# Two transformer blocks on one core: the experts' end reordered with down weights in column halves, and the first projection unit loaded by itself

## The chip, the cores and the metric

The kernel runs on one core of a Trainium2 chip, in float32, as one program of five instruction streams: TensorE (PE in the profile, PEld for its weight loads), VectorE (DVE), ScalarE (ACT), GpSimd (POOL) and SyncE (SP), which here only issues DMAs and waits. The metric is the device time of one execution in microseconds (us), the median of several runs.

## What is computed

```python
def first_block(x, ...):                      # x: 512 tokens x 1024
    h = rms_norm(x, g_attn);  proj = h @ w_in # 1024 x 3072
    o_da = diff_attention(...);  o_sb = stick_breaking(...)
    x = x + concat(o_da, o_sb) @ w_o
    h2 = rms_norm(x, g_ffn)
    return x + hier_moe(h2, wg, bg, we, be, w1, w3, w2)

def hier_moe(h, ...):                         # 4 groups x 8 experts = 32, top 2 of a group
    ...                                       # per expert, on its tokens:
    ys = (silu(xb @ w1[e]) * (xb @ w3[e])) @ w2[e]    # 1024 -> 512 -> 1024
    ys = ys * gate;  out[token] += ys

def second_block(x, c, ctx, ...):             # ctx: 256 x 1024
    h_lat = modulate(rms_norm_2(x, g_pre_mix), sh_m, sc_m)
    p_lat = h_lat @ w_in_2                    # fourier | q_a | kv_a | k_rope
    h_ctx = modulate(rms_norm_2(ctx, g_pre_mix), csh_m, csc_m)
    p_ctx_kv = h_ctx @ w_in_2[:, KV_COL:]     # keys and values of the context
    ...                                       # latent attention, fourier mix, w_out, swiglu
```

## The kernel before

Every weight matrix is cut on the host into items of [128, 4096] float32 (2 MiB, 16 KB a partition). SyncE loads them in one fixed order (`items`) into eight slots: five of the tile `ring`, two halves of `B3` (in the traces `B`), and `TO`. A small loop at the top of the program decides for each item which slot it takes (`where`); before a load SyncE waits until the item that lay in the slot was used (`consumed`). Lines 338 to 365 are that loop, lines 431 to 455 `consumed`.

**The start.** SyncE issues the four parts of x, the parameters PRM and then items 0 to 3. Item 0 is the first quarter of `w_in` that is used; four units of 128 columns are taken from it. For each unit ScalarE rounds the weights (`proj_high`, UH), VectorE takes the rest (`proj_low`, UL), and TensorE multiplies (three products per chunk of 128 rows). The activations are split in the same way: ScalarE makes HH, VectorE HL, from the transposed x in PSUM. `proj_high(0)` waits for the whole item and for PRM.

**The experts.** Each expert x has 64 places for tokens. Its up product takes 16 calls with `w13` (items (x,0) and (x,1), each half of the 1024 rows), two calls at a time side by side in the array. ScalarE makes the silu, VectorE the product (`hidden`), TensorE turns it (`turn`, L957), VectorE copies it (`hidden_cols`, HT). Experts go in pairs p: `down_pair(p)` multiplies experts 2p and 2p+1 with their `w2` items (x,2), 16 calls into PSUM banks 6 and 7, each call 64 rows of one expert. ScalarE and VectorE scale and split the result (YH, YL), and `combine(p, k)` adds it with a one-hot matrix to rows of tokens 128k to 128k+127; VectorE adds that to X (`added`, L2154). `down_pair(p)` stands behind the up product of expert 2p+2, and `combine(p, 0..3)` between the chunks of expert 2p+3's.

**The end of the experts.** After expert 31's up product come its turn, a branch for tokens that found no place (`passes`, not taken here), `down_pair(15)` and `combine(15, 0..3)`. Then the second block starts: keys of the context (`acc` with W1 and `small_keys`, from item `i1`, the first part of `w_in_2`), the norms of X by ScalarE (`row_norm`), and `turn_x(k)`, which turns X and scales it by the norm, in between the small products of the context. With `hT` complete the query projection starts (L57, `ps<-B,ring 128x512`).

The loads end with the `w2` items of experts 30 and 31, then the two parts of `w_in_2` with `w_b_2` in between. Most matmuls are recorded at L57 in the helper `mm`; the tiles tell them apart.

Of the kernel before, what the change touches and what calls it, by code (L numbers as in the profile page):

```python
# [19 lines left out]
NE = 32  # L20
# [5 lines left out]
LN_EXP = 6  # L26
N_PARAM = 927
# [50 lines left out]
def body(nc, ctx, I, out):  # L78
# [95 lines left out]
    PROJ = (3, 4, 5, 2, 0, 1)  # L174
# [73 lines left out]
    WX2 = WX[2].rearrange("p (c n) -> p c n", c=4)  # L248
# [68 lines left out]
    for x in range(NE):  # L317
        use += [(x, 0), (x, 1)]
        if x >= 2 and x % 2 == 0:
            use += [(x - 2, 2), (x - 1, 2)]  # L320
    use += [(NE - 2, 2), (NE - 1, 2)]
    item_of = {u: I_EXP + n for n, u in enumerate(use)}
    for x, part in use:
        items.append(I["w2"][x] if part == 2 else I["w13"][2 * x + part])
    I_IN2 = len(items)
    items += [I["w_in_2"][:, 0:3328], I["w_b_2"], I["w_in_2"][:, 3328:7424]]
# [7 lines left out]

    where, before, landed = [], [], []
# [3 lines left out]
    for i in range(len(items)):  # L339
        if i < I_EXP:  # L340
            line_up = [early[i]]
        if i == I_EXP:
            line_up = [1, 2, 0, 4, 3, NSLOT + 2, NSLOT + 1, NSLOT]
        if I_EXP + 8 <= i <= I_IN2:
            line_up.sort(key=freed.get)
        if i == I_IN2:
            line_up = [k for k in line_up if k < 3]
        if i == I_EXP + 57:
            line_up.remove(NSLOT + 2)
        k = line_up[0]  # L350
        if I_IN2 - 4 <= i < I_IN2:
            k = next(q for q in line_up if (q in (4, NSLOT + 1)) == (i >= I_IN2 - 2))
        line_up.remove(k)
        line_up.append(k)
        if I_EXP <= i < I_IN2:
            x, part = use[i - I_EXP]
            freed[k] = 8 * (x // 2) + 10 if part == 2 else 4 * x + part
# [14 lines left out]
    i1, iw, i0 = I_IN2, I_IN2 + 1, I_IN2 + 2  # L372
# [9 lines left out]
    x_in = [sem(f"x{t}_in") for t in range(4)]  # L382
    prm_in, cst_in, ohb_in, brow_out, tbr_in, zero_out = (
# [27 lines left out]
    up_half = sem("up_half")  # L411
# [30 lines left out]
    def consumed(j):  # L442
# [6 lines left out]
        if j < I_IN2:  # L449
            x, part = use[j - I_EXP]  # L450
            return (up_half, up_mm, dn_mm2)[part], x // 2 + 1 if part == 2 else x + 1
        if j < I_OUT:
            return (kv_mm, 2) if j == i1 else (k_mm, 4) if j == iw else (fi_mm, 4)
# [28 lines left out]
    def sync(e):  # L482
        def load(i):
            e.dma_start(slot_at(i, 0, items[i].shape[1]), items[i]).then_inc(slot_in[where[i]], 16)
# [2073 lines left out]
```

## Time and profile before

| | us |
|---|---|
| median of 3 runs (1482.01 to 1486.90) | 1484.31 |
| the profiled execution's own time | 1481.28 |
| its span | 1479.5 |
| TensorE busy in it | 1413.7 (96%) |
| TensorE waiting for expert weights (three waits) | 7.7 |
| VectorE, ScalarE, GpSimd busy | 595.5, 422.6, 59.2 |

The span is what the profiler saw between the first and the last instruction; the execution's own time is 1.8 us more. The chain that ended last lies for 88% on TensorE and for 6% on DMAs. Busy shares are averages: over slices 11 to 22 of the page's 40 (370 to 814 us, the experts) the DMA engines are at 9 tenths or more and move 427 GB/s, elsewhere mostly under half of that.

### The profile page before, as it was taken

What the parts mean: (1) busy time and instruction counts of PE and PEld (TensorE: products, weight loads), DVE (VectorE), ACT (ScalarE), POOL (GpSimd) and SP (SyncE); (2) the same over time, 40 slices, a digit from 0 to 9 for tenths busy, and PEclk for the clock granted to TensorE, in tenths of its full rate; (3) what the DMA queues carried; (4) which work ended last, traced back from release to release, by engine and by line L of the source; (5) the groups of instructions that cost most, each with busy time, mean ns of one, the idle gap of its engine ahead of it and who ended that gap; (6) DMA issues with size and microseconds to landing.
All of it is one profiled execution on the core that took longest, in us unless ns stands there. A gap on an engine that the chain in (4) does not pass through costs nothing.

```text
span 1479.5 us, 15837 instructions
## 1 busy us (share of the span) xinstructions
PE 1413.7 (96%) x6412; PEld 851.6 (58%) x6412; DVE 595.5 (40%) x1078; ACT 422.6 (29%) x731; POOL 59.2 (4%) x113
## 2 busy tenths in 40 slices
PE   6999999799999999999899899999999999999998
PEld 4777775575433333333333444555457888887886
DVE  4224556735343343333333425276244223223234
ACT  4124765622100100101101323265244222223232
POOL 0000110000210100000000001000000000000000
PEclk9999999999999999999999999999999999999999
DMA  7541117437999999999999511100014223213201
GB/s 318 217 182 57 57 60 316 165 114 296 381 427 427 427 427 426 428 425 427 426 427 428 220 56 58 57 1 1 0 39 189 68 103 114 94 77 114 85 1 57
DMA packets 25762, 302.99 MB, mean 205 GB/s; under 512 B 4188, under 2 KB 4188, under 8 KB 8025
## 3 DMA queue, kind: packets, MB, share of 16 engines
q1 hardware_dynamic: 22984, 297.64, 49.5%
q0 software_dynamic: 2272, 3.52, 0.6%
q8 instruction: 52, 0.85, 0.2%
q10 hardware_dynamic: 432, 0.81, 0.2%
q14 instruction: 22, 0.17, 0.0%
HBM read 301.55 MB, written 4.24 MB: 207 GB/s over the span
## 4 chain that ended last, share of the span: by engine, by line
PE 88%; DMA 6%; DVE 4%; ACT 2%; issue 1%; SPq 0%; POOL 0%; DVEq 0%; ACTq 0%
PE ps L57 83%; DMA ring<-in_w 3%; PE ps L1223 2%; DMA B<-in_w 2%; DMA ring<-in_w_in 1%; PE ps L922 1%; PE ps L957 1%; DVE TMP L2035 0%; PE ps L653 0%; PE ps L835 0%; PE ps L881 0%; DVE UL L1820 0%; ACT TMP L1742 0%; DVE TMP L1823 0%; DVE B L2098 0%
## 5 line engine op out<-in xcount | busy, mean ns | idle before, releaser
L57 PE MATMUL ps<-ring,B 128*64 128x512 f32 (+2 forms) x864 | 230.5, 592 | 4.1 <-DVE B L2098 3.3
L57 PEld LDWEIGHTS ps<-ring,B 128*64 128x64 f32 (+1 forms) x864 | 74.0, 145 | 119.4 <-issue 112.9
L57 PE MATMUL ps<-XH,WH 128*128 128x512 f32 (+1 forms) x368 | 140.9, 383 | 1.3 <-DVE XL L1820 0.7
L57 PE MATMUL ps<-XL,WH 128*128 128x512 f32 (+1 forms) x368 | 139.7, 380 | 0.0
L57 PE MATMUL ps<-XH,WL 128*128 128x512 f32 (+1 forms) x368 | 139.7, 380 | 0.0
L57 PE MATMUL ps<-B 128*64 128x512 f32 (+5 forms) x440 | 117.3, 557 | 0.0
L1820 DVE TENSOR_TENSOR WL<-ring,WH 128x2048 fp32r<-128x2048 f32 x33 | 75.6, 2292 | 95.1 <-ACT WH L1724 95.1
L1724 ACT ACTIVATE WH<-ring 128x2048 fp32r<-128x2048 f32 x33 | 63.2, 1916 | 167.8 <-PE ps L57 167.8
L2154 DVE TENSOR_TENSOR X<-ps,X 128x512 f32<-128x512 f32 x128 | 82.3, 686 | 57.3 <-PE ps L57 57.2
L1550 ACT ACTIVATE TMP<-ps 64x512 f32<-64x512 f32 x32 | 19.0, 594 | 297.9 <-PE ps L57 297.1
L57 PE MATMUL ps<-ring,TMP 128*64 128x512 f32 x336 | 96.6, 615 | 7.3 <-DMA ring<-in_w 4.5
L57 PEld LDWEIGHTS ps<-XH,WH 128*128 128x128 f32 x368 | 69.1, 188 | 16.0 <-DVE XL L1820 1.9
L57 PE MATMUL ps<-B,TMP 128*64 128x512 f32 (+4 forms) x296 | 72.1, 459 | 6.5 <-ACT TMP L1482 5.1
L57 PEld LDWEIGHTS ps<-XL,WH 128*128 128x128 f32 x368 | 69.2, 188 | 13.3 <-issue 0.2
L57 PEld LDWEIGHTS ps<-XH,WL 128*128 128x128 f32 x368 | 69.2, 188 | 13.2
L2405 DVE TENSOR_TENSOR B<-ps,TMP 128x512 f32<-128x512 f32 x22 | 15.2, 692 | 140.7 <-PE ps L57 140.7
L57 PE MATMUL ps<-WH,XH 128*128 128x512 f32 x176 | 68.5, 389 | 1.5 <-DVE XL L1820 1.5
L57 PE MATMUL ps<-WL,XH 128*128 128x512 f32 x176 | 68.5, 389 | 0.0
L57 PE MATMUL ps<-WH,XL 128*128 128x512 f32 x176 | 68.5, 389 | 0.0
L1820 DVE TENSOR_TENSOR UL<-ring,UH 128x1024 fp32r<-128x1024 f32 x32 | 39.1, 1223 | 64.9 <-ACT UH L1358 49.8
L1823 DVE SCALAR_TENSOR_TENSOR YL<-ps,MISC,YH 128x512 fp32r<-128x512 f32 x32 | 22.5, 746 | 104.7 <-ACT YH L1565 104.7
L57 PEld LDWEIGHTS ps<-ring,TMP 128*64 128x64 f32 x336 | 31.0, 141 | 54.8 <-issue 54.8
(317 smaller groups left out, 2182.0 us busy)
## 6 DMA issues: line engine op xcount, KB each, us to landing
ring<-in_w SPq DMA_DIRECT2D x64, 2048.0 KB, 21.5
B<-in_w SPq DMA_DIRECT2D x25, 2048.0 KB, 22.5
ring<-in_w_ada SPq DMA_DIRECT2D x12, 2048.0 KB, 8.2
ring<-in_w_gu SPq DMA_DIRECT2D x11, 2048.0 KB, 8.0
ring<-in_w_in SPq DMA_DIRECT2D x7, 2048.0 KB, 12.3
TO<-in_w SPq DMA_DIRECT2D x7, 2048.0 KB, 15.6
ring<-in_w_down SPq DMA_DIRECT2D x5, 2048.0 KB, 7.2
ring<-in_w_o SPq DMA_DIRECT2D x2, 2048.0 KB, 9.3
```

The source lines that it names most:

```text
L57: return e.matmul(o, l, r, start=first, stop=last, skip_group_check=True)
L922: t = e.transpose(P[n][:, 128 * q:128 * q + 128], XG[:, 128 * c:128 * c + 128], ident)
L957: t = e.transpose(P[4][:, 64 * f:64 * f + 64], HG[x % 2][:, 128 * f:128 * f + 128], ident[0:64, 0:64])
L1223: t = e.transpose(o[:, 128 * c:128 * c + 128], E2[y % 3][:, 128 * c:128 * c + 128], ident)
L1550: e.activation(SL, P[2 + x % 2][64:128, :], ACT.Silu).then_inc(up_sl, 1)
L1724: e.activation(WH[n % 2][:, :].rearrange("p (c n) -> p c n", c=src.shape[1]), src, ACT.Copy).then_inc(ws_hi, 1)
L1820: return e.tensor_tensor(dst, src, high, ALU.subtract)
L1823: return e.scalar_tensor_tensor(out=dst, in0=src, scalar=s, in1=other, op0=ALU.mult, op1=op1)
L2154: e.tensor_tensor(xs, P[h if k % 2 else 6 + h], xs, ALU.add).then_inc(cm_add, 1)
L2405: e.tensor_tensor(aT[:, f, :], P[(2 * f + 4) % 8 + 1 if f else 1], SG[f % 2], ALU.mult).then_inc(at_dve, 1)
```

## The change

1. The `w2` items are cut otherwise. An item holds one half of the output columns for both experts of a pair: (2p, 2) the left 512 columns, (2p, 3) the right. The host stores each expert's halves one behind the other, and the load takes 8 KB a partition from each of two experts. `down_pair(p, h)` is a half of the old one: 8 calls, one bank. Its end raises `dn_half` (h = 0) or `down_mm` (h = 1), and each frees its own slot.
2. The end of the experts has another order. Expert 31's up product follows expert 30's at once; then come both halves of `down_pair(14)`, both turns, `combine_half(14, 0)` and `(14, 1)`, the branch, the context's products, `down_pair(15, 0)`, two small products of the context, `down_pair(15, 1)`, `combine_half(15, 0)` and `(15, 1)`, the context's keys, and the four `turn_x` in a row.
3. The loads follow: expert 31's up weights stand before the halves of pair 14, and the first part of `w_in_2` stands before those of pair 15. The slots of the first loads of the experts are dealt otherwise.
4. VectorE takes the norms' sums of two of the four row blocks of X (`xo_sq`); ScalarE had all four.
5. At the start the first unit of item 0 (columns 0 to 127, stored in one piece) is a load of its own, ahead of PRM; the other three units follow PRM. `proj_high(0)` waits for that load alone, the wait for PRM stands behind it. VectorE scales the second row block of x before it squares the fourth; it squared first before.

```diff
+        if 2 <= x < NE - 2 and x % 2 == 0:
+            use += [(x - 2, 2), (x - 2, 3)]
+    use += [(NE - 4, 2), (NE - 4, 3), (None, None), (NE - 2, 2), (NE - 2, 3)]
...
+            items.append(I["w2"].rearrange("e p (h n) -> h e p n", h=2)[part - 2, x:x + 2].rearrange("r p n -> p r n"))
...
+        e.dma_start(slot_at(0, 0, 1024), items[0][:, 0:1024]).then_inc(unit0_in, 16)
         e.dma_start(PRM[:, 0:N_PARAM], I["PRM"]).then_inc(prm_in, 16)
-        for i in range(4):
+        e.dma_start(slot_at(0, 1024, 4096), items[0][:, 1024:4096]).then_inc(slot_in[where[0]], 16)
+        for i in range(1, 4):
...
+        def down_pair(p, h):
+            i = item_of[2 * p, 2 + h]
+            w = slot_at(i, 0, 4096).rearrange("p (r f n) -> p r f n", r=2, f=4)
+            e.wait_ge(slot_in[where[i]], landed[i])
             e.wait_ge(ht_cp, 2 * p + 2)
             for f in range(4):
+                for r in range(2):
+                    m = mm(e, P[6 + h][64 * r:64 * r + 64, :], HT[r][:, f, :], w[:, r, f, :], f == 0, f == 3)
+            m.then_inc((dn_half, dn_mm2)[h], 1)
+
+        def combine_half(p, h, banks):
+            e.wait_ge(row_set, p + 1)
+            e.wait_ge(yl_set, 2 * p + h + 1)
+            for k, b in enumerate(banks):
+                if p == NE // 2 - 1 and h:
+                    e.wait_ge(cm_add, 8 * p + k + 1)
+                for w, first in ((YH, True), (YL, False)):
+                    m = mm(e, P[b], OHT[p % 2][:, 128 * k:128 * k + 128], w[:, 512 * h:512 * h + 512], first, not first)
+                m.then_inc(tail_mm, 1)
...
+        p = NE // 2 - 2
+        e.wait_ge(cm_add, 8 * p)
+        for h in range(2):
+            down_pair(p, h)
+        turn(NE - 2)
+        turn(NE - 1)
+        combine_half(p, 0, (2, 3, 6, 0))
+        e.wait_ge(ht_cp, NE)
+        combine_half(p, 1, (1, 7, 4, 5))
...
         acc(e, P[2][:, 0:256], [(W1[:, c, 256:384], hcT[:, c, :]) for c in range(8)]).then_inc(cx_mm, 1)
         small_keys(3, hcT, 256).then_inc(cx_mm, 1)
-        turn_x(0)
+        p = NE // 2 - 1
+        e.wait_ge(cm_add, 4 * NE - 8)
+        down_pair(p, 0)
...
+        down_pair(p, 1)
+        combine_half(p, 0, (0, 1, 4, 5))
+        combine_half(p, 1, (0, 1, 4, 5))
...
+        for k in range(4):
+            turn_x(k)
...
+        proj_high(0)
         e.wait_ge(prm_in, 16)
-        proj_high(0)
```

TensorE at the end of the experts, from `combine(14, 3)` on, before (`YH`, `YL` are the parts of a pair's result, `OHT` the one-hot matrices, `B_52` is X's normed diagonal or a slot, `TO,ring` the context's rows and `w_in_2`):

```order
L57 MATMUL ps<-YH,OHT_77 128x512 [waits cm_add]
...
L57 MATMUL ps<-ring,B_52 64x512 x4
L957 MATMUL ps<-CST,TMP 128x64 [waits up_hg,ht_cp]
...
L57 MATMUL ps<-ring,TMP 64x512 [waits slot6_in,slot4_in,ht_cp,cm_add,ov_done]
...
L57 MATMUL ps<-YH,OHT_78 128x512 [waits yl_set,row_set]
...
L57 MATMUL ps<-TO,ring 128x256 [waits cT_dve,slot1_in,cleared]
L57 MATMUL ps<-TO,ring 128x256 x7
L57 MATMUL ps<-TO,ring 32x256 x8
L57 MATMUL ps<-B_52,X 128x128 [waits cm_add,x3_in]
```

The same place now, from pair 14's left half on:

```order
L58 MATMUL ps<-ring,TMP 64x512 [waits ht_cp,slot1_in,cm_add]
L58 MATMUL ps<-ring,TMP 64x512 x7
L58 MATMUL ps<-ring,TMP 64x512 [waits ht_cp,slot2_in]
...
L981 MATMUL ps<-CST,TMP 128x64 [waits up_hg,ht_cp]
...
L58 MATMUL ps<-YH,OHT_77 128x512 [waits yl_set,row_set]
...
L58 MATMUL ps<-TO,ring 128x256 [waits slot0_in,cm_add,cleared,ov_done]
...
L58 MATMUL ps<-ring,TMP 64x512 [waits ht_cp,slot4_in,cm_add]
...
L58 MATMUL ps<-B_52,TMP 64x512 [waits ht_cp,slot6_in]
...
L58 MATMUL ps<-YH,OHT_78 128x512 [waits yl_set,row_set]
...
L58 MATMUL ps<-B_52,X 128x128 [waits cm_add,x3_in]
```

The context's products moved from behind the last `combine` to ahead of the last down pair, a pair's two weight slots are waited for one at a time, and X's turns stand last.

SyncE's last loads before the second block, before:

```order
L484 DMA B_52<-in_w 128x4096 [waits up_mm]
L484 DMA ring<-in_w 128x4096 [waits down_mm] x2
L484 DMA ring<-in_w 128x4096 [waits up_half]
L484 DMA ring<-in_w 128x4096 [waits up_mm]
L484 DMA B_52<-in_w 128x4096 [waits up_mm]
L484 DMA ring<-in_w_in 128x3328 [waits down_mm]
L484 DMA ring<-in_w_b 128x3328 [waits up_half]
```

And now (`128x2x2048` is a column half of two experts):

```order
L497 DMA B_52<-in_w 128x4096 [waits dn_half]
L497 DMA ring<-in_w 128x2x2048 [waits down_mm]
L497 DMA ring<-in_w 128x2x2048 [waits up_half]
L497 DMA ring<-in_w_in 128x3328 [waits up_mm]
L497 DMA ring<-in_w 128x2x2048 [waits up_half]
L497 DMA B_52<-in_w 128x2x2048 [waits up_mm]
L497 DMA ring<-in_w_b 128x3328 [waits dn_half]
```

The load of `w_in_2`'s first part moved ahead of pair 15's two halves, and expert 31's up weights (the first of these rows is their second) ahead of pair 14's.

## Rows read from the trace of the kernel before

**Rows 1.** chain of waits, first 40 us: start, length, what.
```profile
3.55 13.24 DMA ring<-in_w_in
...
19.99 19.70 PE ps L57 x83
```

**Rows 2.** timeline, start: start, length, engine, line, operation, count, idle before.
```profile
12.68 3.71 PE L633 MATMUL ps<-CST,B 128*128 128x128 f32 x24 [0.54 <-DVE B L1835]
12.95 0.20 ACT L1330 ACTIVATE PRM<-PRM 128x1 f32<-128x1 f32 x1
13.19 0.75 DVE L1835 TENSOR_SCALAR B<-X,PRM 128x1024 f32<-128x1024 f32 x1 [0.57 <-ACT PRM L1330]
...
16.87 1.06 ACT L1358 ACTIVATE UH<-ring 128x1024 fp32r<-128x1024 f32 x1 [3.71 <-DMA ring<-in_w_in]
...
17.96 1.23 DVE L1820 TENSOR_TENSOR UL<-ring,UH 128x1024 fp32r<-128x1024 f32 x1 [3.95 <-ACT UH L1358]
19.10 5.35 DVE L1823 SCALAR_TENSOR_TENSOR HL<-ps,PRM,HH 128x512 fp32r<-128x512 f32 x8
```

**Rows 3.** the four DMAs into X, issued 0.82 to 2.20: time to landing.
```profile
DMA to landing us min/median/max: 5.3/7.3/8.5
```

**Rows 4.** busy time by stretch; last columns TensorE clock, DMA share, GB/s.
```profile
20.00:25.00 5.00, 5.00 (x15) 3.96 (x16) 5.00 (x8) 3.49 (x6) 0.00 (x0) 0.66 1.00 424
390.00:395.00 5.00, 5.00 (x26) 1.82 (x27) 0.72 (x2) 0.59 (x1) 0.00 (x0) 1.00 0.88 309
...
750.00:800.00 50.00, 50.00 (x234) 19.42 (x230) 20.56 (x34) 4.32 (x7) 1.95 (x2) 1.00 1.01 427
```

**Rows 5.** load of expert 28's down weights: issue, time to landing.
```profile
L484 SPq DMA_DIRECT2D B<-in_w x1: 328/328/328, 772.6 to 772.6; - x1
...
DMA to landing us min/median/max: 23.8/23.8/23.8
```

**Rows 6.** load of w_in_2's first part: issue, time to landing.
```profile
L484 SPq DMA_DIRECT2D ring<-in_w_in x1: 328/328/328, 808.6 to 808.6; - x1
...
DMA to landing us min/median/max: 16.2/16.2/16.2
```

**Rows 7.** timeline of TensorE, a down pair behind a long wait.
```profile
710.53 8.78 PE L57 MATMUL ps<-ring,TMP 128*64 128x512 f32 x32 [4.54 <-DMA ring<-in_w]
```

**Rows 8.** timeline of TensorE, end of the experts.
```profile
772.35 7.04 PE L57 MATMUL ps<-ring,TMP 128*64 128x512 f32 x32
...
796.68 3.65 PE L57 MATMUL ps<-B 128*64 128x512 f32 x16
801.51 0.61 PE L57 MATMUL ps<-B,TMP 128*64 128x512 f32 x1 [1.18 <-DMA ring<-in_w]
...
808.40 2.77 PE L57 MATMUL ps<-ring,B 128*64 128x512 f32 x12
...
822.61 0.43 PE L957 MATMUL ps<-CST,TMP 64*128 64x64 f32 x4 [1.63 <-DVE TMP L2173]
823.81 1.08 PE L57 MATMUL ps<-ring,TMP 128*64 128x512 f32 x1 [0.77 <-DVE TMP L2179]
...
834.85 0.70 PE L57 MATMUL ps<-YH,OHT 128*128 128x512 f32 x2 [2.44 <-DVE YL L1823]
...
837.39 0.73 PE L57 MATMUL ps<-YH,OHT 128*128 128x512 f32 x2 [0.46 <-DVE X L2154]
...
850.67 2.05 PE L57 MATMUL ps<-B,X 128*128 128x128 f32 x16 [1.48 <-ACT B L1582]
...
856.76 17.40 PE L57 MATMUL ps<-B,ring 128*128 128x512 f32 x40 [0.53 <-issue]
```

**Rows 9.** chain of waits, the last down pair.
```profile
823.81 8.60 PE ps L57 x32
```

**Rows 10.** DMA issues by line: KB each, median us from issue to landing.
```profile
ring<-in_w_down SPq DMA_DIRECT2D x5, 2048.0 KB, 7.2
...
ring<-in_w_down SPq DMA_DIRECT2D x1, 1024.0 KB, 4.6
```

More of the change, by code:

```diff
@@ L26 @@
 LN_EXP = 6
+PROJ = (3, 4, 5, 2, 0, 1)
 N_PARAM = 927
@@ L332, in body @@
     items += [I["w_down_2"][:, 4096 * b:min(4096 * b + 4096, 22528)] for b in range(6)]
+    turns = []
+    for x in range(NE):
+        turns += [(x, 0), (x, 1)]
+        if 2 <= x < NE - 2 and x % 2 == 0:
+            turns += [(x - 2, 2), (x - 2, 3)]
+    turns += [(NE - 4, 2), (NE - 4, 3), (NE - 2, 2), (NE - 2, 3), (None, None)]
+    order = {item_of[u]: n for n, u in enumerate(turns)}
+    FIRST_SLOTS, LAST_SLOTS, LEAVE_TO = [1, 2, 0, 4, NSLOT + 2, NSLOT + 1, 3, NSLOT], (1, 2), I_EXP + 61
     where, before, landed = [], [], []
@@ L342, in body @@
         if i == I_EXP:
[L343 to L344 removed]
+            line_up = FIRST_SLOTS
+        if I_EXP + 8 <= i < iw:
             line_up.sort(key=freed.get)
[L346 to L348 removed]
+        if i == LEAVE_TO:
             line_up.remove(NSLOT + 2)
[L350 to L352 removed]
+        if i == I_OUT:
+            line_up = [where[i1], where[iw], where[i0]]
+        k = LAST_SLOTS[i - i0 - 1] if i >= i0 + 1 - len(LAST_SLOTS) and i <= i0 else line_up[0]
         line_up.remove(k)
         line_up.append(k)
[L355 to L357 removed]
+        if i in order:
+            freed[k] = order[i]
         before.append(max([j for j in range(i) if where[j] == k], default=None))
@@ new lines, in tensor @@
+        for x in range(NE):
+            i, j = item_of[x, 0], item_of[x, 1]
+            w13, b = [slot_at(k, 0, 4096).rearrange("p (w c n) -> p w c n", w=2, c=4) for k in (i, j)], 2 + x % 2
+            if x % 2 == 0:
+                e.wait_ge(ga_xt, x + 2)
+            if x >= 2:
+                e.wait_ge(up_hg, x - 1)
+            e.wait_ge(slot_in[where[i]], landed[i])
+            for c in range(8):
+                if c == 4 and 1 <= x < NE - 1:
+                    turn(x - 1)
+                if 3 <= x < NE - 1 and x % 2 and 3 <= c < 7:
+                    combine(x // 2 - 1, c - 3)
+                if c == 4:
+                    e.wait_ge(slot_in[where[j]], landed[j])
+                xt = XT[x // 2 % 2][:, c, 64 * (x % 2):64 * (x % 2) + 64]
+                mm(e, P[b][64:128, :], xt, w13[c // 4][:, 0, c % 4, :], c == 0, c == 7)
+                m = mm(e, P[b][0:64, :], xt, w13[c // 4][:, 1, c % 4, :], c == 0, c == 7)
+                if c == 3:
+                    m.then_inc(up_half, 1)
+            m.then_inc(up_mm, 1)
@@ L2185, in ctx_cols @@
                                 ALU.mult, ALU.add).then_inc(cT_dve, 1)
-        for x in range(NE + 1):
+        for x in range(NE):
             if x == 24:
@@ L2213, in vector @@
                 e.tensor_copy(IDX, PAIR[:, :, 0]).then_inc(idx_set, 1)
-            if x == NE:
-                passes(v_pass)(e)
             if x >= 2 and x % 2 == 0:
                 rows_of(x // 2 - 1)
-                y_low(x // 2 - 1)
+            if 2 <= x < NE - 2 and x % 2 == 0:
+                if x > 2:
+                    e.wait_ge(cm_mm, 2 * x - 4)
+                for h in range(2):
+                    y_low(x // 2 - 1, h)
             if 4 <= x < NE - 2 and x % 2 == 0:
@@ L2222, in vector @@
                 ctx_cols(4 * (x - 25) + 2)
-        for k in range(4):
-            added(NE // 2 - 1, k)
+        p = NE // 2 - 2
+        e.wait_ge(cm_mm, 4 * p)
+        y_low(p, 0)
+        hidden_cols(NE - 2)
+        hidden_cols(NE - 1)
+        y_low(p, 1)
+        added_half(p, 0, (2, 3, 6, 0))
+        added_half(p, 1, (1, 7, 4, 5))
+        passes(v_pass)(e)
         def turned_rows(k):
```

268 lines of the change are left out of this document (134 added, 134 removed).

## Prediction

> **What bounds the kernel now.** I read the page first: TensorE is busy for 96% of the span and is granted its full clock almost everywhere, so a gain has to come from a place where TensorE waits or where a transfer sets its pace. The list of TensorE's waits names two such places, the first 20 us and the stretch from 800 to 857 us. The chain of waits shows the first: the load of item 0 holds everything for 13.24 us, and TensorE's first projection product starts at 19.99 [rows 1]. The timeline there shows that x is ready long before: ScalarE has the last norm at 13.15, VectorE the last scaled block at 13.94, and then both stand still until the item lands at 16.8 [rows 2]. In the experts the stretches show the DMA engines full (share 1.01, 427 GB/s) [rows 4]. A pair of experts is 12.6 MB, 29.5 us at that rate. Expert 28's down weights, a 2.1 MB load, land at 772.6 + 23.8 = 796.4 [rows 5] and the first part of `w_in_2`, six loads later, at 808.6 + 16.2 = 824.8 [rows 6]: 5 x 2.10 + 1.70 = 12.2 MB in 28.4 us, 4.9 us for a full item and 4.0 for that part. So the stream of weights sets the pace up to pair 15, and TensorE's waits behind the last of them that it waits for are paid in full: 1.18 (weights), 1.63 and 0.77 (turn and copy of expert 31's product), 2.44 (YL), 0.46, 1.48 (norm of a row block) and 0.53 [rows 8]. The down pair at 823.81 takes 8.60 us [rows 9] where another takes 7.04 [rows 8], since the clock fell around it.
>
> **The start.** The four x loads have landed at 2.20 + 8.5 = 10.7 [rows 3]. The new load behind them is 0.52 MB, 1.2 us at 427 GB/s: 11.9. PRM follows at about 13. ScalarE is occupied with x until 13.15 [rows 2], so that is what the first unit waits for now. UH takes 1.06, UL 1.23, the small scaling of the query gain, which now stands in between, about 0.15 (an estimate, a one-column operation), the first HL chunk 5.35 / 8 = 0.67 [rows 2], handovers together 0.2: 13.15 + 3.3 = 16.5, against 19.99 before, so **3.4 us**. The other condition is X turned: the last block is scaled at 13.94 and its first chunk needs one of 24 turns of 3.71 / 24 = 0.15 us: 14.1, not late. Behind the first product HL delivers a chunk every 0.67 us and TensorE needs three records of 19.70 / 83 = 0.24 for it [rows 1], so nothing falls back. Unit 1 needs the rest of item 0, at 16.8 as before, for the same bytes stand ahead of it, and ScalarE comes to it only after eight HH. TensorE ran at 0.66 of its clock between 20 and 25 us [rows 4], after its wait; I keep that stretch as it is. Everything behind follows TensorE, the experts' loads too, since each is released by a product, so I let the 3.4 us reach the end. Bounds: 1.5 (a slow DMA start, PRM late) to 4.5.
>
> **Column halves of the down weights.** TensorE can start a pair when the left half has landed, 4.9 us before the right one. At 710.53 it waited 4.54 us for both [rows 7]. But the gain there is handed back: the bytes are the same, the stream is full, and TensorE only waits for a later item instead. What counts is when the last item arrives that TensorE waits for. Two small effects on the stream remain. In 390 to 395 us the DMA engines were at 0.88 [rows 4], for lack of a free slot; the left half now frees its slot 3.5 us earlier (half of 7.04). That is worth up to 0.12 x 5 = 0.6 there and some more in the next stretch; I take **0.5 us**, bounds 0 and 1.5. And the half items are 8 KB a partition instead of 16. The last `w_down` load is such a one: 1.05 MB in 4.6 us, against 7.2 for 2.10 MB in 16 KB rows [rows 10]. With 4.9 us of the 7.2 for the bytes at 427 GB/s, 2.3 are fixed and 2.3 remain for 1.05 MB: not slower. I take nothing.
>
> **The end of the experts.** New landings, counted in the old time: 796.4 and 801.3 (expert 31's up weights), 806.2 and 811.1 (pair 14, left and right), 815.1 (`w_in_2`), 820.0 and 824.9 (pair 15). Expert 30's product ends at 800.3 (796.68 + 3.65) [rows 8], or earlier by what the halves saved. Expert 31's takes 2 x 3.65 and cannot pass 801.3 with its second half: about 805.1. The left half of pair 14 starts at 806.4, the right one at **811.3**. That is the last wait for weights: pair 15's halves are wanted at about 825 and 829.5.
>
> What stands behind is TensorE's own work. Between 801.51 and 856.76 lie 55.2 us. Waits in it: 1.63 + 0.77 + 2.44 + 0.46 + 1.48 + 0.53 = 7.3. Low clock: 8.60 - 7.04 = 1.6. Work: 46.3 us, the same instructions in both kernels. Of these, expert 31's product (7.3) and pair 14's left half (3.5) lie ahead of 811.3, so 35.5 follow. New waits in it: the branch's flag is now read without a wait beside it (0.3, an estimate; the wait of 0.77 covered it before), each product of `combine_half(15, 1)` waits for the addition that frees its bank, and these start late by VectorE's YL (0.5), and the first `turn_x` waits for the last addition and ScalarE's norm (0.5); both are estimates between the waits for VectorE and ScalarE of before, 0.46 and 1.48, so together the new waits have the bounds 0.5 and 3. The other old waits go because something stands beside them: the copy of expert 31's product beside expert 30's turn and the additions, YL of a left half beside the right half's products, of pair 15's right half beside `combine_half(15, 0)`, the norms of blocks 1 to 3 beside the turns before them. 811.3 + 35.5 + 1.3 = 848.1 against 856.76: **8.7 us**. ScalarE is the next to be late: it must have the last block's fifth chunk when the query product comes to it, 4 x 2 x 17.40 / 40 = 3.5 us into that product [rows 8]. The copies of the context's keys moved behind, and TensorE asks for them only after two products of 7 us.
>
> **The clock at the end.** The three short waits for weights at 800, 805 and 810 us have a like in the trace: behind 1.18 us of waiting the pair ran at full speed (801.51 to 808.40 is 6.9) [rows 8], behind 4.54 it took 8.78 instead of 7.04 [rows 7]. The new waits are about 1.3 us each, like the first, but three stand close together, and what falls behind 811.3 costs 1.7 us. I take **0.5 us** of loss, bounds 0 and 3.5. The Trainium skill, "TensorE: Matmul & The Clock Gate", section "HAM oscillation — how this bites in real kernels", speaks against this change: short bursts of products between waits for DMAs keep the array at the lower clock again and again. By it both halves of pair 14 would run at 1.2 GHz, and the right one alone adds 3.5; the wait of 1.18 in this trace did not do that.
>
> **Sum.** -3.4 - 0.5 - 8.7 + 0.5 = -12.1. From the profiled execution's own time that is 1481.28 - 12.1 = 1469.2. That execution was 3.0 us faster than the median of the runs, and as the changed kernel is judged by its runs I start from 1484.31: **1472.2 us**.
>
> **Rivals.**
> (a) The waits in front of pair 14 bring the clock down, and the low stretch reaches over its right half and the turns and sums behind: 2 x 1.7 = 3.5 us instead of 0.5. For it: 8.60 and 8.78 above. Against: the pair at 801.51. Time 1475.
> (b) The change doesn't do what it says at the start: the small load does not land ahead, since the DMA engines work at several loads at a time, or the earlier start is eaten by low clock. Against: x, in four equal loads, landed one after the other (5.3 to 8.5 us) [rows 3]. Time 1484.3 - 8.7 = 1475.6.
> (c) Slower: the column halves load at a lower rate. 32 of them are 67.1 MB, 157 us of a stream without slack, so every loss of rate is paid at once: the gain of 12 is gone below 67.1 / (157.2 + 12.1) = 396 GB/s, and the kernel is slower by over 0.3% below 67.1 / 173.8 = 386 GB/s. At 350 GB/s it is 192 us, 35 more: 1507. For it: every second 8 KB is skipped and two experts are read at a time, which no load of before does. Against: rows 10. The Trainium skill's "DMA: Bandwidth & Descriptors", section "Latency and other measured facts", tells of copies that fall to half rate when the rows lie large powers of two apart; its smallest such distance is 512 KiB, here rows lie 16 KiB apart and only the two experts 2 MiB. No row here shows such a load.
> (d) More: low clock falls away at the start too (a third of 5 us, 1.7), and the stream gains 1.5: 1469.5.
>
> **Chances.** Forecast 0.60, its own range 1468 to 1476; (a) 0.14, (b) 0.08, (c) 0.09, half of it slower, (d) 0.09. A difference under 0.3% (4.5 us) is about what a measurement of this kernel can't tell from none. Faster: the forecast, (a), (b), (d) less some room for runs that differ among themselves: 0.87; same 0.07; slower 0.06. Range: the forecast's, plus (d), (a) and (b), and part of (c): 1466 to 1479.
>
> **What would show it.** TensorE's first projection product at about 16.5. A load of a column half in 4.9 us and 427 GB/s through the experts; at 400 or less, (c). Waits of TensorE for weights many and small, the last one in front of pair 14's right half, none for pair 15. From the end of that wait to the query product 36.8 us; more with a clock under 1.0 in it is (a). The query product begins 12 us earlier than before, and from there the two traces run in parallel. I am wrong if TensorE waits for pair 15's weights, or if a wait on YL or an addition stands in the new order with over 1 us.

## The result, and the profile after

| | before | after |
|---|---|---|
| median of the runs (lowest to highest) | 1485.61 (1482.01 to 1488.45, 4 runs) | 1471.84 (1467.53 to 1473.27, 4 runs) |
| the profiled execution's own time | 1481.28 | 1473.27 |
| its span | 1479.5 | 1471.5 |
| TensorE waiting for expert weights | 7.7 | 10.9 |

The ratio of the runs is 0.9907, 95% interval 0.9887 to 0.9927: 13.8 us faster (11 to 17), where the prediction said 1472.2. The two profiled executions differ by 8.0 us only. The one of before was faster than each of the four timed runs, the one of after is the slowest of its four. One reason why runs of one kernel differ is stretches in which TensorE is granted the lower of its two clock levels (1.2 GHz); one of them costs about 1.7 us (0.83 of the clock over the 10 us from 820 on in the kernel before).

Every run has a mean granted clock. What is missing to 1, times the span, is an estimate of the time that low clock cost it. It is 11 to 12 us in the mean over 45 runs of the kernel before, and 6.2 over the four of the changed kernel. So some 5 of the 13.8 us are fewer low stretches, and the other 9 come from elsewhere.

**The start.** The end of the chain of waits of the changed kernel in the first 40 us (start, length, what), against [rows 1]:

```profile
10.58 5.33 PE ps L648 x25
...
15.99 0.70 ACT HH L1403
...
16.71 0.76 DVE HL L1872
...
17.61 18.07 PE ps L58 x83
```

The load of 13.24 us is gone from it. In its place stand the load of x, its norms and then the turns of x on TensorE. The timelines of ScalarE and VectorE there show that the new load did its part (start, length, engine, line, operation, count, idle before), against [rows 2]:

```profile
13.44 1.04 ACT L1397 ACTIVATE UH<-ring 128x1024 fp32r<-128x1024 f32 x1
15.99 1.85 ACT L1403 ACTIVATE HH<-ps,PRM 128x512 fp32r<-128x512 f32 x3 [1.51 <-PE ps L648]
```

```profile
14.51 1.23 DVE L1869 TENSOR_TENSOR UL<-ring,UH 128x1024 fp32r<-128x1024 f32 x1 [0.20 <-ACT UH L1397]
...
16.71 2.73 DVE L1872 SCALAR_TENSOR_TENSOR HL<-ps,PRM,HH 128x512 fp32r<-128x512 f32 x4 [0.91 <-ACT HH L1403]
```

UH starts at 13.44, right behind the last root, and UL ends at 15.74. But HH, which the forecast had ready long before, waits 1.51 us for TensorE, and HL 0.91 for HH. The first product comes at 17.61, 2.4 us earlier than before and not 3.4.

The turns of x alone (stretch, its length, TensorE busy with them and how many, granted clock, DMA share, GB/s), first in the changed kernel, then in the kernel before:

```profile
10.58:15.51 4.93, 4.93 (x24) 1.00 1.05 429
15.51:16.50 0.99, 0.99 (x10) 1.00 1.04 439
```

```profile
12.68:14.44 1.76, 1.76 (x9) 1.00 1.00 428
14.44:16.20 1.76, 1.76 (x17) 1.00 1.03 438
```

In both a turn starts 0.21 us behind the one ahead at first, and 0.11 us from 15.5 and 14.4 us on. Half the pace is what the lower clock level would give; that it is the clock is concluded from the pace alone, for the clock column reads 1.00 here.

**The experts.** Stretches of the changed kernel (the last three numbers are TensorE's granted clock as a share of full, the share of the DMA engines, GB/s), against [rows 4]:

```profile
20.00:25.00 5.00, 5.00 (x22) 3.18 (x21) 3.69 (x6) 1.68 (x3) 0.00 (x0) 1.00 1.01 428
390.00:395.00 5.00, 5.00 (x26) 1.72 (x24) 0.68 (x1) 0.59 (x1) 0.00 (x0) 1.00 0.94 324
450.00:600.00 150.00, 150.00 (x694) 57.06 (x692) 56.04 (x92) 14.20 (x22) 11.68 (x12) 1.00 1.01 425
750.00:800.00 50.00, 50.00 (x230) 18.96 (x230) 20.54 (x35) 3.75 (x6) 1.73 (x2) 1.00 1.01 425
```

The same long stretch in the kernel before:

```profile
450.00:600.00 150.00, 150.00 (x696) 56.83 (x694) 54.69 (x90) 14.13 (x23) 10.69 (x11) 1.00 1.01 427
```

The low clock of 20 to 25 us (0.66 before) is gone. This goes with the first load: the profiled executions of all three kernels with the old start have 0.66 there, behind 2.8 to 3.8 us without work for TensorE, and all ten with the new load have 1.00, behind 0.9 to 1.1 us. The DMA engines are as full as before, yet they move 425 GB/s and not 427. By the landings of single loads in the trace a whole item (16 KB a partition in one run) lands 4.90 us after the one ahead, in both kernels; a column half (two runs of 8 KB) 4.97.

**The end of the experts.** TensorE in the changed kernel, against [rows 8]:

```profile
801.94 3.65 PE L58 MATMUL ps<-B 128*64 128x512 f32 x16 [0.62 <-DMA B<-in_w]
806.93 3.65 PE L58 MATMUL ps<-ring,TMP 128*64 128x512 f32 x16 [1.34 <-issue]
811.84 3.65 PE L58 MATMUL ps<-ring,TMP 128*64 128x512 f32 x16 [1.25 <-DMA ring<-in_w]
...
819.85 4.62 PE L58 MATMUL ps<-TO,ring 128*128 128x256 f32 x32
824.39 3.65 PE L58 MATMUL ps<-ring,TMP 128*64 128x512 f32 x16
...
829.16 3.65 PE L58 MATMUL ps<-B,TMP 128*64 128x512 f32 x16
...
835.08 0.47 PE L58 MATMUL ps<-YH,OHT 128*128 128x512 f32 x1 [0.23 <-DVE X L2221]
...
839.55 7.66 PE L58 MATMUL ps<-B,X 128*128 128x128 f32 x64 [0.32 <-ACT B L1630]
847.05 3.17 PE L58 MATMUL ps<-B,ring 128*128 128x512 f32 x7
```

811.84 is the right half of pair 14, behind its weights (1.25). Pair 15's halves at 824.39 and 829.16 wait for nothing. The waits of 1.63, 0.77, 2.44, 0.46 and 1.48 of before have shrunk to 0.23 and 0.32. The query product starts at 847.05, 9.7 us earlier. The low stretch of the kernel before at 820 to 830 is gone too: with the old end of the experts all four profiled executions have one between 823 and 835, with the new end none of nine has one there. Two waits that the trace calls "issue" are waits for weights as well: they end where a load lands, 4.9 us behind the one ahead, and only the landing's record is missing (806.93, 1.34). TensorE's list of waits (us in total, times, longest):

```profile
PE ps L58 <- DMA ring<-in_w: 7.2, 6, 2.8
...
PE ps L58 <- DMA B<-in_w: 2.0, 3, 1.1
...
PE ps L58 <- issue: 1.6, 2, 1.3
```

That is 7.2 + 2.0 + 1.6 = 10.9 before rounding, in eleven waits. Before there were three: 1.97, 4.54 and 1.18.

### The profile page after: what moved, and what is told of

Its sections match the earlier page's. It is cut to its first block, busy times and chain, and to the rows that moved or that the text cites. A ratio compares the mean times of both kernels' runs of the same rounds, so it can differ in the third digit from the quotient of the medians.

```text
span 1471.5 us, 15850 instructions
## 1 busy us (share of the span) xinstructions
PE 1412.0 (96%) x6412; PEld 849.4 (58%) x6412; DVE 598.5 (41%) x1082; ACT 421.8 (29%) x727; POOL 59.1 (4%) x113
## 4 chain that ended last, share of the span: by engine, by line
PE 86%; DMA 7%; DVE 4%; ACT 2%; issue 1%; SPq 0%; POOL 0%; DVEq 0%; ACTq 0%
PE ps L58 81%; DMA ring<-in_w 7%; PE ps L1258 2%; PE ps L937 1%; PE ps L981 1%; DVE TMP L2085 1%; DMA X<-in_x 0%; PE ps L648 0%; PE ps L668 0%; PE ps L850 0%; PE ps L896 0%; ACT TMP L1791 0%; DVE TMP L1872 0%; DVE TMP L2088 0%; DVE B L2148 0%
## 5 line engine op out<-in xcount | busy, mean ns | idle before, releaser
L58 PE MATMUL ps<-B 128*64 128x512 f32 (+5 forms) x456 | 121.2, 559 | 0.9 <-DMA B<-in_w 0.9
L2204 DVE TENSOR_TENSOR X<-ps,X 128x512 f32<-128x512 f32 x112 | 72.2, 687 | 64.0 <-PE ps L58 64.0
L58 PE MATMUL ps<-ring,TMP 128*64 128x512 f32 x336 | 75.2, 594 | 8.2 <-DMA ring<-in_w 6.6
L58 PEld LDWEIGHTS ps<-B 128*64 128x64 f32 (+2 forms) x456 | 39.6, 151 | 42.2 <-issue 36.3
L58 PE MATMUL ps<-B,TMP 128*64 128x512 f32 (+4 forms) x280 | 55.5, 439 | 6.4 <-ACT TMP L1521 5.1
```

What stands on the lines that cost most here:

```text
L58: return e.matmul(o, l, r, start=first, stop=last, skip_group_check=True)
L2204: e.tensor_tensor(xs, P[h if k % 2 else 6 + h], xs, ALU.add).then_inc(cm_add, 1)
```

## The experiments

Each ran in five rounds, against the kernel before on the same chip; ratios are to before, with their 95% intervals.

### The start alone

```diff
+        e.dma_start(slot_at(0, 0, 1024), items[0][:, 0:1024]).then_inc(unit0_in, 16)
         e.dma_start(PRM[:, 0:N_PARAM], I["PRM"]).then_inc(prm_in, 16)
-        for i in range(4):
+        e.dma_start(slot_at(0, 1024, 4096), items[0][:, 1024:4096]).then_inc(slot_in[where[0]], 16)
+        for i in range(1, 4):
             load(i)
...
+        proj_high(0)
         e.wait_ge(prm_in, 16)
-        proj_high(0)
```

> The kernel before with the start of the change alone: the first projection unit's 512 KB loaded by itself ahead of the vector of parameters, its split first on ScalarE and VectorE, the weights of that slab laid out by unit; experts as before. Theory A (two gains that add): the first product starts at 17.6 us as in the changed kernel (19.99 before), the stretch of low clock at 22 to 26 us is gone, and the end comes 2.4 to 4 us earlier: ratio 0.9973 to 0.9984. Rival B (the start is taken back where the experts are fed by the transfers, which run at their full rate from 400 us on and end no earlier): TensorE waits for weights more, and the end is within 1 us of before, ratio 0.9993 or more. Together with the run that has the end alone this must add up to the 13.8 us of the whole change; 2 us or more missing would mean that the parts act on each other.

Measured: 1481.18 (1477.95 to 1484.54, 12 runs), before 1483.70 (23 runs), ratio 0.9973 (0.9958 to 0.9988), 4.0 us by the ratio. Its first product is at 17.77, and the clock of 20 to 25 us is full. Theory A holds, the start is not swallowed in the experts: the gain lasts to the end.

### The start's load without the start's orders

```diff
+        e.wait_ge(prm_in, 16)
         proj_high(0)
-        e.wait_ge(prm_in, 16)
```
(against the start alone; VectorE's order as before too)

> The kernel before with one part of the start's change: the first unit's 512 KB loaded by itself ahead of the parameters. Not moved: ScalarE waits for the parameters ahead of the unit's UH, VectorE scales the tiles in the old order and does its factor ahead of UL. Theory M (the load is the whole of it): the unit lands at 12.4, the parameters at 13.5, so UH starts at 13.6 in place of 13.44, and the first product comes at 17.5 to 17.9 as with the whole start: ratio to before 0.9973 to 0.9985. Rival N (the orders carry half or more of it): first product at 18.5 or later, ratio 0.9987 or more.

Measured: 1478.59 (1477.87 to 1480.17), before 1484.58, ratio 0.9957 (0.9942 to 0.9972). The first product is at 17.36:

```profile
17.36 0.47 PE L58 MATMUL ps<-HH,UH 128*128 128x512 f32 x1 [0.89 <-DVE HL L1830]
```

So the load is the whole of it; the orders add nothing that can be seen. The run looks better than the one with the whole start, but the intervals meet, and the traces show what lies between the two profiled executions (spans 1476.1 and 1477.4). This is 260 to 280 us, first with the whole start, then with the load alone:

```profile
260.00:280.00 20.00, 15.69 (x104) 8.49 (x96) 14.72 (x62) 12.68 (x43) 0.00 (x0) 0.91 0.59 213
```

```profile
260.00:280.00 20.00, 15.43 (x109) 9.51 (x101) 16.23 (x69) 14.67 (x48) 0.00 (x0) 1.00 0.58 213
```

One has a low stretch there, the other none; with it TensorE reaches the first expert's product at 361.33 against 359.37. The timed runs differ in the same way: by their mean clocks low clock cost 10.7 us with the whole start and 7.6 with the load alone. Executions of the same code differ in this too: the changed kernel's profiled one has the stretch at 260 to 280, the one with the keys behind pair 15 (below), the same code up to 800 us, has not.

### The end alone

The changed kernel with the start's lines of the diff taken back.

> The changed kernel with its start undone: only the column halves, the new order at the end of the experts and the context's keys inside. Theory A: the query product 9 to 10 us earlier than before's 856.76, and the time 10 to 11.5 us under before's: ratio 0.9923 to 0.9933. Rival B (the start is swallowed in the experts): this kernel alone has all of the change, 13.8 us, ratio 0.9907. Rival C (the halves' slower transfers bind here, since the experts stand later against them): less than 9 us, and TensorE waits for weights less than the changed kernel's 9.2 us, as the experts start 2.4 us later against the same stream.

Measured: 1475.51 (1474.25 to 1476.81), before 1483.70, ratio 0.9936 (0.9916 to 0.9956), 9.5 us by the ratio. 0.9973 x 0.9936 = 0.9909, and the whole change has 0.9907: the two gains add, and rival B falls. Theory A's size was a little too large: it had 10 to 11.5 us, and the query product 9 to 10 us earlier, where it is at 849.72, 7.0 earlier. Of that 1.7 is a low stretch at 284 us that the profiled execution of before has not. Rival C isn't settled: 9.5 us is over its 9, but the interval is 6.5 to 12.5, and the waits for weights (8.5, and 1.6 under "issue") are a little shorter than with the earlier start, as it says.

### The shape of the loads alone

```diff
-        items.append(I["w2"][x] if part == 2 else I["w13"][2 * x + part])
+        if part == 2:
+            y = x - x % 2
+            items.append(I["w2"].rearrange("e p (h n) -> h e p n", h=2)[x % 2, y:y + 2].rearrange("r p n -> p r n"))
```

> The kernel before, with nothing changed but the shape of the down weights' loads: each 2 MB load takes one column half of two experts (two pieces of 8 KB for each partition) instead of all columns of one expert (one piece of 16 KB). TensorE's order, the slots and their release as before. Theory D (the halves are a little slower to load): in the changed kernel such a load lands 4.96 to 4.97 us after the one ahead, a whole one 4.89 to 4.90, so 32 loads cost 32 x 0.07 = 2.2 us of the stream; here the loads of the halves land 4.96 apart too, the last up weights' landing moves from 801.3 to 803 or later, and the end comes 1 to 2.2 us later (ratio 1.0007 to 1.0015). Rival E (the prediction's: no slower): spacing 4.89, the end within 0.5 us.

Measured: 1487.43 (1485.91 to 1488.16, 12 runs), before 1483.70, ratio 1.0018 (1.0005 to 1.0030): 2.7 us slower. Halves land 4.97 us apart, whole items 4.90. TensorE's waits for weights (7.7 before):

```profile
PE ps L57 <- DMA ring<-in_w: 8.2, 4, 3.0
...
PE ps L57 <- DMA B<-in_w: 3.7, 2, 2.1
```

Theory D holds, if with more than its 1 to 2.2 us (the interval is 0.7 to 4.5), and E (the prediction's) falls.

### The halves in one run each

```diff
-            items.append(I["w2"].rearrange("e p (h n) -> h e p n", h=2)[part - 2, x:x + 2].rearrange("r p n -> p r n"))
+            items.append(I["w2p"][x + part - 2])
```

> The changed kernel with each load of a down half stored in one run in memory (16 KB for each partition, an array of its own beside the one that the overflow pass reads), everything else as it is. Theory D (two pieces of 8 KB for each partition make a load 0.07 us longer): spacing back to 4.89, pair 14's right half lands 2 us sooner, TensorE's waits for weights shrink from 9.2 us, and the time falls by 1 to 2.2 us against the changed kernel's 1471.8: 1469.6 to 1470.8. Rival E (the spacing comes from what the other queues do meanwhile, or from the slot in which a load lands): spacing stays 4.96 and the time too. Rival F: spacing falls but the time doesn't, as the wait moves to other work.

Measured: 1469.47 (1467.27 to 1470.50), before 1483.70, ratio 0.9892 (0.9873 to 0.9912). The difference of 2.2 us to the changed kernel (0.9907) is as expected, but by the ratios alone it is inside the intervals. The stretch of the experts has its old rate:

```profile
450.00:600.00 150.00, 150.00 (x694) 57.01 (x692) 56.04 (x92) 14.20 (x22) 11.68 (x12) 1.00 1.01 427
```

TensorE's waits for weights are down from 10.9 to 7.8 (5.1 + 1.1 + 0.3, and one of 1.3 under "issue").

### All loads of the experts in two runs

```diff
-            items.append(I["w13"][2 * x + part])
+            items.append(I["w13p"][2 * x:2 * x + 2, :, 2048 * part:2048 * part + 2048].rearrange("r p n -> p r n"))
```

> The changed kernel with the 64 loads of up weights in two pieces of 8 KB for each partition too (from an array of its own), so that all 96 loads of the experts have this shape; what is computed and where it lies in SBUF stay. Theory D (two pieces cost a load 0.07 us): a whole load in the changed kernel is 4.90, here 4.97, some 60 of them ahead of the last wait for weights make the stream 4 us longer, TensorE waits for weights by about that much more (10.9 us in the changed kernel with the waits whose releaser the profile doesn't tell), and the time rises by 3 to 4.5 us to 1475 to 1476.5. Rival O (it is the reading from two experts' places 2 MB apart, or the slots of these loads, and not the number of pieces): spacing stays 4.90 for the up loads, the time within 1 us.

Measured: 1475.84 (1474.10 to 1476.51), before 1484.58, ratio 0.9936 (0.9921 to 0.9951), 4 us more than the changed kernel. All loads land 4.97 apart, and TensorE waits 14.9 us for weights (10.9 + 4.0):

```profile
450.00:600.00 150.00, 150.00 (x696) 57.33 (x694) 56.70 (x92) 14.20 (x22) 11.70 (x12) 1.00 1.01 420
```

### The halves in four runs each

```diff
-            items.append(I["w2p"][x + part - 2])
+            j, g = (x + part - 2) % 4, (x + part - 2) // 4 * 4
+            items.append(I["w2p"][g:g + 4, :, 1024 * j:1024 * j + 1024].rearrange("a p n -> p a n"))
```
(against the halves in one run each)

> The kernel with down halves in an array of their own (e4_whole), each load in four pieces of 4 KB for each partition in place of one of 16 KB. Theory D (a cost for each piece): one piece 4.90, two 4.97, so four 5.1 us; 30 such loads ahead of the last wait make 6 us of stream, and the time rises by 5 to 6 us against e4_whole, to 1474.5 to 1475.5. Rival P (a cost that comes once, as soon as a load isn't one run): four pieces land 4.97 apart as two do, and the time is the changed kernel's, 1471 to 1472.

Measured: 1475.86 (1475.05 to 1476.57), before 1484.58, ratio 0.9936 (0.9921 to 0.9952), 6.4 us more than with one run, where 5 to 6 were expected. These loads land 5.10 apart, the whole ones beside them 4.90, and from 450 to 600 us the DMA engines move 420 GB/s, as with all loads in two runs.

One, two and four runs a partition: 4.90, 4.97, 5.10. Each further run costs a load of 2 MiB 0.07 us, and rival P falls. Every further run also lay 2 MiB from the last in memory, in all these kernels; whether two runs close by would cost the same stays open.

### The keys behind pair 15

```diff
-        acc(e, P[2][:, 0:256], [(W1[:, c, 256:384], hcT[:, c, :]) for c in range(8)]).then_inc(cx_mm, 1)
-        small_keys(3, hcT, 256).then_inc(cx_mm, 1)
         p = NE // 2 - 1
         e.wait_ge(cm_add, 4 * NE - 8)
         down_pair(p, 0)
         down_pair(p, 1)
         combine_half(p, 0, (0, 1, 4, 5))
         combine_half(p, 1, (0, 1, 4, 5))
+        acc(e, P[2][:, 0:256], [(W1[:, c, 256:384], hcT[:, c, :]) for c in range(8)]).then_inc(cx_mm, 1)
+        small_keys(3, hcT, 256).then_inc(cx_mm, 1)
```

> The changed kernel with one part of the tail undone: the context's 32 key products and the two small ones that follow stand behind pair 15's products and sums again, its four products with the key-value weights between the second and third turn of the rows; the order of the loads, the column halves and the combination by halves stay. Theory G (the keys are what TensorE does while pair 15's halves land): in the changed kernel these land at 820.8 and 825.7 us, and TensorE is done with pair 14 at 819.85, so without the keys it waits 0.95 us for the first half, about 1.2 us for the second, and for YH and YL some tenths more; the query product comes at 849.3 to 850.3 in place of 847.05, the time 2.2 to 3.2 us over the changed kernel's. Rival H (only the halves matter, the place of the keys doesn't): within 0.7 us of the changed kernel, no wait for pair 15's weights of over 0.5 us.

Measured: 1476.02 (1474.58 to 1477.23), before 1485.50, ratio 0.9938 (0.9920 to 0.9956): 4.2 us over the changed kernel by the medians. The place of the keys matters, and by more than theory G said; but the cause that it gave was wrong. TensorE at the two places:

```profile
809.03 3.65 PE L58 MATMUL ps<-ring,TMP 128*64 128x512 f32 x16 [1.26 <-DMA ring<-in_w]
...
819.74 3.65 PE L58 MATMUL ps<-ring,TMP 128*64 128x512 f32 x16 [2.55 <-DVE X L2223]
...
839.65 5.41 PE L58 MATMUL ps<-B,X 128*128 128x128 f32 x32 [2.50 <-ACT B L1632]
```

The wait in front of pair 15 is 2.55 us for VectorE's last sums of pair 14 (X, L2223), not for weights. And the turns of X stand 2.50 us behind ScalarE's norm, which had the four key products beside it before. From pair 14's right half to the query product it is 850.20 - 809.03 = 41.2 us in place of 35.2. Of these 6.0 us, 1.7 are a low stretch that falls on the turns (838 to 844 us, granted clock 0.72) and 4.3 the waits. Whether that stretch belongs to the waits ahead of it or is chance stays open. VectorE's and ScalarE's orders were moved with the keys, so this is the price of the whole arrangement.

The same rows show how far executions of one code lie apart: up to the right half of pair 14 this kernel is the changed kernel, and it gets there at 809.03, the changed kernel's profiled execution at 811.84.

### An eighth less to load

```diff
-            items.append(I["w13"][2 * x + part])
+            items.append(I["w13"][2 * x + part][:, 0:3584 if x >= 8 else 4096])
```

> Leaves work out: from the ninth expert on each load of up weights brings 3584 of its 4096 columns, so the products read old numbers in the rest; everything else as in the changed kernel. 48 loads are an eighth shorter, 29 us of the stream. Theory I (TensorE's 9.2 us of waits for weights in the changed kernel, and they alone, are what the transfers still cost it from there on): these waits all but vanish, those ahead of the ninth expert stay, and the time falls by 7 to 9 us, to 1463 to 1465; 35 us from the start of pair 14's right half to the query product stay 35. Rival J (the waits are only where TensorE waits first, and the same time is lost to the engines behind it, YL, the sums and the turned rows): the waits for weights vanish, others grow, and the time falls by under 3 us.

Measured: 1458.24 (1458.04 to 1459.11), before 1485.50, ratio 0.9820 (0.9801 to 0.9840): 13.6 us under the changed kernel, where 7 to 9 were expected. Theory I is right in kind and its size was too small. Of the waits for weights none is left, not 9.2 us but 10.9 of them, for I had counted without the "issue" ones. The query product is at 831.93:

```profile
804.73 4.62 PE L58 MATMUL ps<-TO,ring 128*128 128x256 f32 x32
...
831.93 17.33 PE L58 MATMUL ps<-B,ring 128*128 128x512 f32 x40
```

That is 15.1 us earlier than after's. 2.2 of it are there at the first expert already (358.96 against 361.18: the low stretch at 260 to 280 again, and a first product at 16.95 and not 17.61). The other 12.9 all come in at the eleven waits, which cost 2.0 more than their 10.9 us of idle time. Behind a wait TensorE's products don't overlap with those ahead: from the left half of pair 14 to the turns behind the right one it takes 815.42 - 806.93 = 8.49 us in the changed kernel, 800.32 - 793.35 = 6.97 here, 1.52 for a recorded wait of 1.25. From the context's products to the query product it is 27.2 us in both. So the transfers still cost this kernel some 12.9 us.

### TensorE kept busy before the turns of x

```diff
         e.wait_ge(cst_in, 16)
+        for n in range(16):
+            e.transpose(P[7][:, 0:128], ident, ident)
```
(on top of the halves in one run each)

> The kernel with the down halves stored in one run (e4_whole) and 16 idle turns of the identity on TensorE ahead of the turns of x, from the landing of the constants at about 7 us to about 10.5. Theory K (the first turns of x are slow because TensorE stood idle before, and it is they that ScalarE's HH waits for): a turn of x takes 0.12 us from the start in place of 0.17 to 0.19 in the mean, HH starts at 15 or before, and the first product comes when UL is done, at 16.5 us in place of 17.0 to 17.6; the time falls by 0.5 to 1.1 us against e4_whole. Rival L (the turns wait for the scaled rows, not for TensorE's pace): HH and the first product where they were, and no gain.

Measured: 1467.84 (1467.13 to 1470.34), before 1485.50, ratio 0.9889 (0.9868 to 0.9909); without the idle turns 0.9892. TensorE and then ScalarE at the start:

```profile
10.79 4.82 PE L648 MATMUL ps<-CST,B 128*128 128x128 f32 x32
16.75 0.47 PE L58 MATMUL ps<-HH,UH 128*128 128x512 f32 x1 [1.14 <-DVE HL L1872]
```

```profile
14.95 3.00 ACT L1403 ACTIVATE HH<-ps,PRM 128x512 fp32r<-128x512 f32 x5 [0.32 <-PE ps L648]
```

HH starts at 14.95, against 15.99 in the changed kernel and 15.37 in the kernel that this one is built on. HL now waits for UL, and the first product is at 16.75 against 17.61 and 16.99. In part this is chance. The turns change their pace at 12.7 us here; in the six executions with this start and without idle turns that is anywhere from 13.6 to 15.5, HH starts at 15.05 to 15.99, and the first product comes at 16.66 to 17.61. The earliest of them is the kernel with the keys behind pair 15:

```profile
16.66 0.47 PE L58 MATMUL ps<-HH,UH 128*128 128x512 f32 x1 [0.95 <-DVE HL L1874]
```

So the pace of the turns sets HH wherever it changes late, and the first half of theory K holds in kind; the turns took 0.15 us in the mean (4.82 / 32), not 0.12 from the start. With idle turns it changed earlier in both executions that have them (12.7 and 12.0). The gain in time can't be told from none.

> e7_warm with one thing more: the third tile of x is scaled by VectorE (0.72 us) and not by ScalarE (1.15 us), so ScalarE gets to the fourth tile's root and to UH sooner. Theory K: with the turns out of the way, UH starts at 12.9 in place of 13.44, UL ends about 15.2, and the first product comes at about 16.0: 0.5 us less than e7_warm, 1 to 1.6 less than e4_whole. Rival L: the first product at 16.5 to 17 as in e7_warm.

The third tile of x on VectorE in place of ScalarE. Measured: 1468.94 (1465.46 to 1472.17), ratio 0.9886 (0.9865 to 0.9907). The first product is at 16.52, with UH at 13.35 though x landed 0.36 us later than in the run before (ScalarE starts on it at 7.35, not 6.99); UH at 12.9 and the product at 16.0, as theory K has it, did not come; the medians tell nothing apart. Inconclusive.

The best versions are those with the halves in one run each, with or without the idle turns: 1467.84 to 1469.47, about 16 us under before by the ratios.

## Why the prediction was right, and where not

The time (1472.2 against 1471.84) is right and the mechanism in the main too, but that they meet within 0.4 us is luck. The sum said 12.1 us less than 1484.31; the kernel before has 1485.61 with its fourth run, and the gain was 13.8. The base was 1.3 too low and the gain 1.7 too small. Within the gain the term for the column halves was wrong in sign and the one for the end too small.

- **Start, 3.4 us predicted.** The load landed as forecast. UH started at 13.44 and not 13.15, and UL ended at 15.74; with the small scaling (to 15.80), 0.76 for HL and 0.14 to the product this alone gives 16.7, 0.2 behind the forecast. The other 0.9 are HL's wait for HH. The step that failed is "X turned ... 14.1, not late". It took the 24 turns at 0.155 us from a row of before [rows 2], and that row mixes two paces: 0.21 us until 14.4, 0.11 from then on. Eight turns had come before it there, and the fourth tile was scaled late enough for TensorE to be free. Now all 32 run in one piece from 10.58, at 5.33 / 25 = 0.21 us for those that the first HH needs, and end behind the data. How much that costs depends on when the pace changes: with the same code the first product came between 16.66 and 17.61. The low clock of 20 to 25 us, which I had kept, fell away and gave back more than was missing (rival d's first half): at 35.68 the next stage starts 4.0 us earlier than the 39.69 of [rows 1] (19.99 + 19.70). Measured alone: 4.0 us, 1.8 to 6.2. Rival (b) is refuted by that and by the first product.
- **Column halves, 0.5 us gained predicted.** Wrong in sign. The stall at 390 us went as forecast (0.88 to 0.94), but "not slower" was read off one load of 1 MiB beside idle queues [rows 10], a time to landing with 2.3 us of fixed part in it; it can't show 0.07 us. 32 halves at 0.07 are 2.2 us, and the stream is full, so they are paid: 2.7 us (0.7 to 4.5) by the shape alone. It is rival (c) in small: 422 GB/s for a half (2.097 MB in 4.97 us), where 396 would have eaten the gain. The Trainium skill, "DMA: Bandwidth & Descriptors", section "Latency and other measured facts", has the half rate only for rows 4 MiB and more apart; at 512 KiB its copies had 207 GB/s of 214, at 2 MiB 164. The two experts of a load lie 2 MiB apart here, and nothing like a loss of that size was seen. The same page of the Trainium skill, section "Specifications", asks for 512 B or more for full rate; the runs here are 8 and 4 KB, and each further one still cost 0.07 us.
- **End of the experts, 8.7 us.** The structure held: small waits for weights, the last in front of pair 14's right half, none for pair 15, no wait for YL or a sum over 1 us. From there to the query product it took 35.2 us where 36.8 were predicted: the "new waits" of 1.3 us came to 0.23 + 0.32, the work to 34.7 and not 35.5. The clock stayed full, so neither the loss of 0.5 us nor rival (a) came. The step "By it both halves of pair 14 would run at 1.2 GHz" read too much into the Trainium skill, "TensorE: Matmul & The Clock Gate", section "HAM oscillation — how this bites in real kernels": in its case the waits are longer than the bursts of products between them, here waits of 0.62 to 1.34 us stand beside halves of 3.65.
- **Where the end stands.** Pair 14's right half started at 811.84, where the forecast with its own start and stream has 811.3 - 3.4 - 0.5 = 807.4. Of these 4.4 us, 1.0 was missing at the first expert already: 361.18 against 363.55 is 2.4 us and not 3.4, for the start had brought 4.0 and the low stretch at 260 to 280, which the profiled execution of before has not, took 1.7. About 2.1 are the 30 halves ahead; the other 1.3 are not placed. 4.4 late and 1.6 + 0.5 short make the query product 2.3 us later than the forecast, 9.7 earlier and not 12. The end alone, halves included, measured 9.5 us (6.5 to 12.5), of which the keys' place is some 4, where the forecast had 8.7; without the halves' price it would be 2 more. So this term was too small: by the runs' mean clocks low clock cost 8.4 us with the new end and 11.2 in the kernel before on the same chip, and the forecast had counted one stretch of 1.6.
- **The parallel behind 847.** Not quite: the changed kernel's execution has another low stretch at 870 to 890, so that its end is 8.0 us earlier and not 9.7:

```profile
870.00:890.00 20.00, 17.90 (x50) 6.61 (x43) 9.79 (x15) 5.05 (x9) 4.39 (x6) 0.91 0.28 105
```

- **The base.** I started from the median of the runs and not from the profiled execution, from which the same sum gives 1469.2. The traces' own difference of 8.0 us would have given 1476.3.

## What to carry to other kernels

Where a stream of transfers is full, count every load's cost to a hundredth and keep what it brings to a partition in one run: 0.07 us for a second run, 96 times, is half of what the reordering here gains. A wait is best filled with work from the next stage that is ready: the keys' products in front of pair 15 covered sums and norms that no one had thought of as late, worth about 4 us, and when such work is moved, look for those other engines and not only for the load. When an edit brings a stage forward, ask again what is late there; the engine that had time before may be the one that sets the pace.

## What the runs showed of the hardware

- A load of 2 MiB into 128 partitions, with the queue full: 4.90 us in one run of 16 KB a partition, 4.97 in two, 5.10 in four. A second run a partition is 128 more in all, 8 for each of 16 DMA engines if they are shared out evenly: about 9 ns each (an estimate).
- Stretches at the lower of TensorE's two clock levels (1.2 GHz) come and go between executions of the same code: at 260 to 280 us a granted clock of 0.91 over 20 us in one, 1.00 in another, about 1.7 us each. Profiled executions of the kernels here have between one and five such stretches, so two traces can differ by some us through these alone. Others belong to the code: at 20 to 25 us behind 2.8 to 3.8 us without work in three of three executions with the old start and none of ten with the new.
- TensorE's first turns of x, from 10.6 us on, start 0.21 us apart and then, from one turn to the next, 0.11. With the same code the change came between 13.6 and 15.5 us in six executions, with 3.5 us of idle turns ahead at 12.7 and 12.0. The clock column shows nothing of it.
- Waits for weights of 0.62, 1.34 and 1.25 us, 4.9 us from one to the next, left the clock at full: it is 1.00 from 800 to 848 us, where the kernel before had 0.95 from 811 on.
